# Layer 1's gate products of two branches in Strassen's form: seven block products of 256 columns per pair of column tiles

## The reference, cut to what matters

```python
cq, ckv, kr, glu, dq, dk, dv, gates = split_cols(h @ w_in)     # gates: 3 * 1024 columns
...
g = jax.nn.sigmoid(gates).reshape(*gates.shape[:-1], N_BRANCH, D_MODEL)
y = (g[..., 0, :] * (o_mla @ w_o_mla) + g[..., 1, :] * (o_conv @ w_o_conv)
     + g[..., 2, :] * (o_diff @ w_o_diff))
return y @ w_out
```

## Time and profile before

| what | value |
|---|---|
| time of three runs | 1473.99, 1475.76 (median), 1480.12 us |
| span of the profiled execution | 1474.6 us; that is the profiled execution's own time, no other is recorded for it |
| PE busy | 1391.2 us, 94% |
| DVE, ACT, POOL busy | 783.0 (53%), 366.1 (25%), 175.2 us (12%) |
| granted TensorE clock, mean | 0.986 |
| chain that ended last | PE 80%, DMA 10%, DVE 4% |

### The profile page before, as it was taken

One profiled execution on the slowest core, in us unless ns is written; L12 is line 12 of the kernel. 1 busy time (PEld: TensorE's weight loads), 2 busy tenths in 40 slices (PEclk: granted clock), 3 DMA queues, 4 the chain that ended last, 5 costly groups with the idle time before them and its releaser, 6 DMA issues.

```text
span 1474.6 us, 19245 instructions
## 1 busy us (share of the span) xinstructions
PE 1391.2 (94%) x7494; PEld 799.9 (54%) x7494; DVE 783.0 (53%) x1738; ACT 366.1 (25%) x795; POOL 175.2 (12%) x118
## 2 busy tenths in 40 slices
PE   6999999999999999989998878999999999999876
PEld 3444444554444445655554437744677885666543
DVE  2579944568887963433132117894753443444322
ACT  4112314432223012222222224141542202100001
POOL 0021521000011210012221210152000110000000
PEclk9999999999999999999999999999999999999999
DMA  9303120144535348199999978232533478999996
GB/s 386 156 36 110 62 101 13 58 143 157 185 112 203 125 194 351 72 349 417 419 418 420 416 272 350 94 114 79 206 116 143 159 300 365 402 419 420 421 420 249
DMA packets 59550, 347.65 MB, mean 236 GB/s; under 512 B 8388, under 2 KB 15172, under 8 KB 28352
## 3 DMA queue, kind: packets, MB, share of 16 engines
q1 hardware_dynamic: 53856, 335.86, 57.5%
q0 software_dynamic: 5024, 8.40, 1.5%
q10 hardware_dynamic: 576, 2.10, 0.4%
HBM read 343.44 MB, written 11.80 MB: 241 GB/s over the span
## 4 chain that ended last, share of the span: by engine, by line
PE 80%; DMA 10%; DVE 4%; SPq 2%; ACT 2%; issue 1%; DVEq 0%; POOLq 0%; ACTq 0%
PE bank L442 75%; DMA arena<-w_up_in 9%; ACT arena L1289 2%; PE bank L788 2%; SPq L2939 1%; DVE arena L1750 1%; PE bank L542 1%; PE bank L1163 1%; SPq L2953 1%; DMA x<-x_in 0%; DMA arena<-y 0%; DVE am L2036 0%; PE bank L1183 0%; SPq L2905 0%; DVE arena L2138 0%
## 5 line engine op out<-in xcount | busy, mean ns | idle before, releaser
L442 PE MATMUL bank<-arena 128*128 128x512 f32 (+12 forms) x5944 | 1227.5, 441 | 23.7 <-DMA arena<-w_up_in 13.1
L442 PEld LDWEIGHTS bank<-arena 128*128 128x128 f32 (+4 forms) x5944 | 661.3, 161 | 503.3 <-issue 385.7
L1289 ACT ACTIVATE arena<-bank 128x512 f32<-128x512 f32 (+5 forms) x423 | 202.3, 499 | 913.5 <-PE bank L442 802.6
L1750 DVE SCALAR_TENSOR_TENSOR arena<-arena,bank 64x256 f32<-64x256 f32 (+2 forms) x121 | 57.8, 479 | 253.1 <-ACT arena L1289 182.1
L1750 DVE SCALAR_TENSOR_TENSOR arena<-arena,early 128x512 f32<-128x512 f32 (+1 forms) x254 | 177.5, 771 | 0.4
L2036 DVE TENSOR_REDUCE am<-bank 128x1 f32<-128x512 f32 (+1 forms) x96 | 55.5, 599 | 129.9 <-PE bank L442 129.8
L2723 POOL TENSOR_TENSOR arena<-arena 128x512 f32<-128x512 f32 (+1 forms) x32 | 37.3, 1168 | 438.4 <-DVE arena L1750 438.4
L1289 ACT ACTIVATE arena<-bank,am 128x512 f32<-128x512 f32 (+1 forms) x96 | 58.6, 613 | 82.0 <-DVE am L2039 81.8
L2762 POOL DMA_INDIRECT y<-arena,routing x33 | 33.0, 999 | 180.2 <-ACT arena L1289 180.2
L788 PEld LDWEIGHTS bank<-con,arena 128*128 128x128 f32 x240 | 29.8, 141 | 35.2 <-issue 22.4
L788 PE MATMUL bank<-con,arena 128*128 128x128 f32 x240 | 38.6, 275 | 4.8 <-DVE arena L2051 4.7
(11 more groups left out here) (226 smaller groups left out, 824.0 us busy)
## 6 DMA issues: line engine op xcount, KB each, us to landing
arena<-w_gate_in SPq DMA_DIRECT2D x60, 1024.0 KB
arena<-w_up_in SPq DMA_DIRECT2D x60, 1024.0 KB
arena<-w_down_in SPq DMA_DIRECT2D x45, 1024.0 KB, 14.9
arena<-mg_in SPq DMA_DIRECT2D x12, 2048.0 KB, 7.8
arena<-adaT_in SPq DMA_DIRECT2D x40, 512.0 KB, 3.7
arena<-adaT_in SPq DMA_DIRECT2D x16, 1024.0 KB, 7.4
arena<-ada_in SPq DMA_DIRECT2D x6, 2048.0 KB, 15.2
arena<-mo_in SPq DMA_DIRECT2D x6, 2048.0 KB, 8.3
```

Of the source, the lines that this page charges most:

```text
L442: return nc.tensor.matmul(out, w, rhs, start=start, stop=stop)
L1289: return nc.scalar.activation(out, in_, fn, **kw)
L1750: return V.scalar_tensor_tensor(out, in0, sc, in1, op0=op0, op1=op1)
```

## The change

For two column tiles (a group g: c = 2g and 2g+1), the weights are four blocks w11, w12, w21, w22 (column tile by half of the row tiles), and `h` four blocks h11, h12, h21, h22 (half of the row tiles by context or latent tokens). Before, the group is 16 matmuls of 512 columns. After, it is seven products q, x, r, 11, 12, y, z, each 4 matmuls of 256 columns, of sums of the blocks, and the four output blocks are put together from them. This holds for b = 0 and b = 1 in layer 0; the third branch and layer 1 of the code stay as they were. The slices per unit become 5, 5, 5, 5, 6, 6, 6, 5, 5, ... of the smaller matmuls for b = 0 and 14 for b = 1 in place of 8 large ones. `ada_units` and `ada_finish` calls leave `merge_steps`; in the program before they issue nothing there.

New work on the other engines: POOL forms four sums of blocks of `h` once (128x1024 each) and, per group, four sums of weight blocks (128x512; `sums_ahead`, `sums_behind`) and two sums of outputs (128x256; `upper`, `corner`). ACT copies q and x out of PSUM and does the tanh of both tiles when the group is complete. DVE takes r, 11, 12, y and z out of PSUM (128x256 each), in `merge_tiles`. The mean of the convolution's norm moves from a unit 2 to 3.

```diff
-        GATES, ALL = KD * KD, KD * KD + 4 * KD
+        GATES, ALL = (7 * 16, KD * KD), (7 * 16 + 4 * KD, KD * KD + 4 * KD)
...
-                n = [3, 3, 2] * 8 + [4] * 8 + [8] * 8 + [4] * 8
+                n = [5] * 4 + [6, 6, 6, 5, 5] + [5, 4, 4, 4] * 3 + [5, 4, 4] + [4] * 8 + [14] * 8 + [4] * 8
...
+                def group_step(b, g, i):
+
+                    p, k = divmod(i, 4)
...
+                    w11, w12, w21, w22 = w[:, c, 0:4], w[:, c, 4:8], w[:, c + 1, 0:4], w[:, c + 1, 4:8]
+                    first, second = slice(0, CTX), slice(CTX, T)
+                    name, cls, lhs, rhs = (("q", "a", w11, h[:, 0:4, first]), ("x", "a", w21, h_sums[0]), ("r", "d", weight_sum, h_sums[1]),
+                                           ("11", "d", w12, h[:, 4:8, first]), ("12", "d", w11, h[:, 4:8, second]),
+                                           ("y", "d", w21, h_sums[2]), ("z", "d", w22, h_sums[3]))[p]
+                    if k == 0:
+                        begin(cls, (name, l, b, g))
+                        if name in "x r 12 y".split():
+                            pe.wait_ge(sums_ready, pool_sums({"x": "s1", "r": "s2", "12": "s4", "y": "s3"}[name], b, g))
+                    ins = mm(bank_of[(name, l, b, g)][:, 0:256], lhs[:, k, :], rhs[:, k, :], k == 0, k == 3)
...
+                def gates_tanh(b, g):
+
+                    t1, t2 = gate_tiles(b, g)
+                    act.wait_ge(empty["d"], Dn[("z", l, b, g)])
+                    f(t1[:, :], t1[:, :], ACT.Tanh, scale=0.5)
+                    act.wait_ge(sums_ready, pool_sums("corner", b, g))
+                    f(t2[:, :], t2[:, :], ACT.Tanh, scale=0.5).then_inc(gates_done, 1)
...
+                    if p == 2:
+                        ps = take(("r", l, b, g))
+                        dve.wait_ge(empty["a"], A[("q", l, b, g)])
+                        give(V.tensor_tensor(t2[:, 0:256], t1[:, 0:256], ps[:, 0:256], op=SUB))
+                    elif p == 3:
+                        ps = take(("11", l, b, g))
+                        give(V.tensor_tensor(t1[:, 0:256], t1[:, 0:256], ps[:, 0:256], op=ADD))
+                    elif p == 4:
+                        ps = take(("12", l, b, g))
+                        dve.wait_ge(sums_ready, pool_sums("u", b, g))
+                        give(V.tensor_tensor(t1[:, 256:512], t1[:, 256:512], ps[:, 0:256], op=ADD))
+                    elif p == 5:
+                        ps = take(("y", l, b, g))
+                        give(stt(t2[:, 0:256], ps[:, 0:256], -1.0, t2[:, 0:256], MUL, SUB))
+                    elif p == 6:
+                        ps = take(("z", l, b, g))
+                        dve.wait_ge(sums_ready, pool_sums("corner", b, g))
+                        give(V.tensor_tensor(t2[:, 0:256], t2[:, 0:256], ps[:, 0:256], op=SUB))
...
+                def sums_ahead(b, g):
+
+                    n_, w11, _, w21, w22 = group_weights(b, g)
+                    pool.wait_ge(ring_ready[n_ % NRING], 16 * (n_ // NRING + 1))
+                    G.tensor_tensor(w21, w21, w22, op=ADD).then_inc(sums_ready, 1)
+                    pool.wait_ge(sums_ready, pool_sums("s1", b, g))
+                    if (b, g) != (0, 0):
+                        pool.wait_ge(full["d"], Dn[("r", l) + ((b, g - 1) if g else (b - 1, 3))])
+                    G.tensor_tensor(weight_sum, w11, w21, op=ADD).then_inc(sums_ready, 1)
...
+                def sums_behind(b, g):
+
+                    _, w11, w12, w21, w22 = group_weights(b, g)
+                    pool.wait_ge(full["a"], A[("q", l, b, g)])
+                    G.tensor_tensor(w11, w12, weight_sum, op=ADD).then_inc(sums_ready, 1)
+                    pool.wait_ge(full["a"], A[("x", l, b, g)])
+                    G.tensor_tensor(w21, weight_sum, w22, op=SUB).then_inc(sums_ready, 1)
...
+                    for n in range(1, 8):
+                        sums_behind(n // 4, n % 4)
+                        upper(n // 4, n % 4)
+                        if n < 7:
+                            sums_ahead((n + 1) // 4, (n + 1) % 4)
+                        corner(n // 4, n % 4)
```

More of the change, by code:

```diff
@@ L255, in attn_units, with pool_sums @@
                     [(i, t, seen[t]) for i in range(HD) for t in tiles])
-        GATES, ALL = KD * KD, KD * KD + 4 * KD
+        GATES, ALL = (7 * 16, KD * KD), (7 * 16 + 4 * KD, KD * KD + 4 * KD)
+        PRODUCTS = 7
+        def pool_sums(what, b, g):
+            n = 4 * b + g
+            if what == "corner":
+                return 6 * n + (9 if n < 7 else 7)
+            if n == 0 and what in ("s1", "s2"):
+                return {"s1": 2, "s2": 3}[what]
+            return 6 * n + {"s1": 1, "s2": 2, "s4": 4, "s3": 5, "u": 6}[what]
         MERGE = (1, 0, 2)
@@ L1535, in gates @@
                             gate(b, c)
-                        elif what == "ada":
-                            ada_raw(c)
+                        elif what == "product":
+                            group_tile(b, *c)
+                        elif what == "gates":
+                            gates_tanh(b, c)
                         elif (what, b, c) == ("branch", 0, KD - 1) and not columns[l]:
@@ L2077, in branch @@
                     ps = take(("branch", l, c, b))
[L2078 removed]
+                    if l == 0 and b < 2:
+                        dve.wait_ge(gates_done, 4 * b + c // 2 + 1)
+                    else:
+                        dve.wait_ge(empty["a"], A[("gate", l, c, b)])
                     out = yt[c][:, q0:T] if b == 0 else gt8[:, c, q0:T]
@@ L2153, in merge_tiles @@
                             branch(b, c)
-                        elif what == "adaT":
-                            ada_finish(c)
+                        elif what == "product":
+                            group_tile(b, *c)
                 peak_a(0)
```

116 lines of the change are left out of this document (84 added, 32 removed).

## The result

The changed kernel takes 1497.48 us, median of 4 runs (1497.05 to 1500.64), against 1477.94 us for the kernel before (4 runs, 1473.99 to 1481.83). The ratio is 1.0142, with an interval of [1.0112, 1.0171]: slower by 1.4%. The profiled execution took 1497.79 us with a span of 1495.9, which is 21.3 more than the span of before. Two executions of the study stand apart, one of the kernel before at 1842 us and one of the split read-outs at 7984 us; neither enters a ratio, and no run says what held them up.

A forecast was written before the change was run, and what follows sets the result against it. The prediction took PE to bound the kernel. From a span of 1474.6, -5.2 (a units), +6.4 (loop), +11 (port), +1 (column load) and +0.8 (d units 8 to 15) gave 1488.6, so 1490 us, range 1474 to 1504.

The forecast's parts named there:

- The signs: Expected in d units 0 to 7: PE gaps ahead of y, longer unit pairs, DVE passes about 2.3 us; 256-column records at 0.220.
- a units, -5.2: First branch (b = 0): smaller products save PE 5.9 us, less 0.7 given back for single late maxima.
- The loop, +6.4: d units 0 to 7: PE and DVE wait on each other, 19.2 us per group instead of 17.6, four groups 76.8.
- the port, +11: d units 0 to 7: 22 POOL additions each cost DVE 0.5 us on the port they share.
- y and z on PE 3.5: Loop step in d units 0 to 7: multiplying y and z takes PE 3.5 us per group.
- Column load, +1: Before d unit 4's second column: DVE wants the load at about 8.2 us, while it came at 9.2.
- d units 8 to 15, +0.8: From d unit 8: DVE starts 2.8 us behind PE instead of 1.5, costing 0.8 us.
- Block sums of `h`, 0: POOL's four early additions, 9.4 us from 49.2, end ahead of the convolution chain and cost nothing.
- Rival (a): d units 0 to 7: loop binds but POOL's additions cost DVE nothing, 11 less, 1479 us; chance 0.18.
- Rival (b): d units 0 to 7: read-outs in time, 11 by 4.6 us of the unit, PE stays the bound, 1464 us; chance 0.10.
- Rival (c): a units stall too, nearly each of 22 units losing 0.6 us: +13 on the forecast, 1503 us; chance 0.09.
- the +23 of my bound: d units 0 to 7: upper bound of the port's price, each of 22 POOL additions delaying DVE by its whole length.

The follow-up runs named there:

- e1: Changed kernel with the seven products for b = 0 only, b = 1 multiplied as before: 1469.5 us, ratio 0.9958 to the kernel before.
- e2: Changed kernel with POOL's additions of b = 1 cut to 8 elements: stretch d 0 to d 8 85.8 us against 94.8; 1523.7 us, not compared.
- e4: Changed kernel plus twenty unread 128-column matmuls on PE behind each product 12 of b = 1: 1489.9 us, ratio 1.0095 to before.
- e10: Changed kernel, odd d units reading 11 and 12 before the first column, y and z between columns, plus twelve unread matmuls behind 12: 1487.6 us.
- e5: Changed kernel with DVE's conditioning columns next to d units 0 to 7 cut to 8 elements: stretch d 0 to d 8 64.9 us against 94.8.
- e12: Changed kernel, one column in d units 1, 3, 5, 7, behind all read-outs; two in d 8, last fold omitted: 1491.1 us; kernel before with this table 1484.6.
- e13: Changed kernel, one column in d units 1, 3, 5, 7, between read-outs of 12 and y; two in d 8, last fold omitted: 1483.7 us; control 1484.6.

## Why the prediction was right, and where it was off

The mechanism is the forecast one: y waits for DVE's read-out of 11, DVE waits for y and z, and the a units gain. The signs that it named are there in kind, but most are larger or smaller than it said: PE's gap ahead of y is 4.1 to 6.6 us and not 2 to 5, the pairs of units take 22.5 to 24.5 us and not 19 to 23, the delayed passes take 1.74 to 2.12 us and not 2.3, and the records of y and z are not at 0.220. By its terms:

- **a units, -5.2.** Measured -5.2: 6.9 at d unit 0, less the 1.7 of the shorter steps ahead. In e1, another execution with the same a units, it is 4.5.
- **The loop, +6.4, and the port, +11.** The 19.2 us a group plus the port's 11 give 87.8 us for the four groups where 96.6 was measured (94.8 and the 1.8 ahead). With 8.0 of clock taken off, 88.6 are left, so the two terms together were 0.8 short. One by one they were further off: e2's groups take 87.5 us without the port, 78.7 without the 8.8 of its clock, so the loop is 1.9 above 76.8, and the port is 9.9 of time in the loop, 1.1 below 11. Of DVE's own time the port takes 11.1: the excess over e2's durations is 15 x 0.195 and 15 x 0.117 in the passes, 4 x 0.79 in the folds, 4 x 0.31 and 4 x 0.19 in the scaled copies of L2115, and 1.3 in smaller ones. That 11 came so near is partly luck, since I priced column passes alone, and 6.4 of the 11.1 fall on other steps, down to a fold of 128x8.
- **The clock, missing: 8.0.** I took "y and z on PE 3.5" from rows at full clock, although the same forecast has PE idle for 2 to 5 us just before. This is the step that failed: y and z ran at a granted clock of 0.57 to 0.70 and took 8.0 us more in the four groups; e4 gives it back by keeping PE at work.
- **Column load, +1.** Nothing: no column waits for its load in the stretch. The loop was slower than forecast, which fits: with a faster loop e10 waits 1.07 us.
- **d units 8 to 15, +0.8.** d unit 15 opens 22.1 us later than before, d unit 8 21.0: 1.1.
- **Block sums of `h`, 0.** The first a unit of the stretch opens 0.3 us later (220.18 and not 219.92); the -5.2 of the a units has this in it.

The sum 1488.6 - 1 (load) + 8.0 (clock) + 0.8 (loop and port) + 0.3 (d units 8 to 15), less 0.8 that come back behind d unit 15, is 1495.9, the span.

Rival (a), a free port, is out by e2. Rival (b), read-outs in time, fails at its own condition: DVE reads 11 at 389.26, 10.4 us into unit 3, not at 4.6; e5 shows that with DVE's columns out of the way it comes near. Rival (c) is out: the a units keep PE busy 78.3 of 78.8 us.

On the rule of the Trainium skill (SBUF — State Buffer, Who interferes with whom): this stretch agrees with it. The pass at 381.60 took 1.74 beside POOL's 1.55 and 2.24, beside POOL's 1.26 at 384.53 L2094 took 0.64 and not the 0.17 that it takes in e2, and the maxima were not held, as it says of reductions. But DVE lost 11.1 us to the 22 additions, some 0.5 each, and never came near the "whole length" for each that made the +23 of my bound.

One simpler view would have told the sign, given the price of the port. Before, DVE had 57.0 of the 66.9 us (the window at the head of the experiments). The change adds some 8 us of read-outs and 11 of port, and one column of 2.4 us falls outside the stretch (15 and not 16): DVE's own work of 72.6 us is above the 66.9 that the stretch took, before any wait is counted. PE saved 4 us there (66.9 to the 62.9 of e5) and could not have kept them. The view works in one direction only: in e2, e12 and e13 DVE's work of 61.5 to 64.7 us would have fitted into 66.9, and the stretch was still 85.8, 81.2 and 75.6.

## What to carry to other kernels

When a change takes work from the busiest engine and gives some to the second, add the new work to the second's busy time in each stretch, port waits included, and compare it with the old length of the stretch. If it is longer, the change loses; if it is shorter, the waits that the order leaves open still decide (e2, e12, e13). The part that gains, here the first branch, can be had alone. In a loop that closes over two engines, try long filler work in the wait for the other engine first; here that beat the place ahead of the read-out that releases it and the one behind the last read-out. Price matmuls that follow an idle gap at the lower clock as well, and look whether work that nobody reads is cheaper than the gap.

## What the hardware showed

- **Clock after a gap.** With 4.1 to 6.6 us of idle before them, the 16 records of y and z ran at a mean granted clock of 0.57 to 0.70 and took 5.2 to 6.4 us, not 3.7; after a gap of 2.18 us behind extra matmuls they ran in 3.72. The length of the gap alone does not tell: in e12 a gap of 3.54 us left the clock at 1.00 and the 16 records at 3.72 us (at 405.72), in e13 one of 2.39 brought 0.70 and 5.20 us (at 400.26). The levels are 1.2 and 2.4 GHz; a mean between them says that the clock changed on the way.
- **The smallest steps wait too.** A DVE step of 128x4 lasted as long as a whole addition of POOL beside it. DVE and POOL in the kernel after, next to the block sums of `h`:

```profile
52.40 2.08 DVE L1955 TENSOR_SCALAR early<-early 128x124 f32<-128x124 f32 x1
54.52 2.33 DVE L1956 TENSOR_SCALAR early<-early 128x4 f32<-128x4 f32 x1
...
59.38 0.17 DVE L1956 TENSOR_SCALAR early<-early 128x4 f32<-128x4 f32 x1
```

```profile
52.05 2.35 POOL L2767 TENSOR_TENSOR down_more<-arena,down_more 128x1024 f32<-128x1024 f32 x1
54.48 2.35 POOL L2768 TENSOR_TENSOR down_last<-arena 128x1024 f32<-128x1024 f32 x1
...
83.51 10.01 POOL L2772 TENSOR_TENSOR arena<-arena 128x512 f32<-128x512 f32 x1 [24.25 <-ACT small L1322]
```

The same step takes 0.17 us without POOL and 2.33 with it. At 83.51 it is POOL that waits: its addition lasts 10.01 us beside a chain of DVE steps, against 1.26 alone. What decides who gives way there was not tried.
